# The last rows of a decoder block: norm vector multiplied in ahead, rstd and residual in one vector operation per half row

## The reference

```python
def rms_norm(x, g):
    xf = x.astype(jnp.float32)
    y = xf * lax.rsqrt(jnp.mean(xf * xf, axis=-1, keepdims=True) + EPS)
    return (y * g.astype(jnp.float32)).astype(x.dtype)
...
        h = rms_norm(x, g_pre_mlp[l]) * (1.0 + sc2) + sh2
        y = jnp.square(jax.nn.relu(h @ w_fc1[l])) @ w_fc2[l]
        x = x + gt2 * rms_norm(y, g_post_mlp[l])
```

## Time and profile before

| what | us |
|---|---|
| median of 3 runs (1533.65 to 1534.89) | 1533.8 |
| the profiled execution | 1535.47 |
| its span on the core | 1533.7 |
| PE busy in the span | 1429.6 |
| DVE busy | 1093.5 |
| ACT busy | 637.0 |
| POOL busy | 633.0 |

### The profile page before, as it was taken

How to read it: one execution, slowest core, us unless ns; L and a number is a source line. 1 busy time by engine, 2 the same in 40 slices (tenths; PEclk the granted TensorE clock), 3 DMA queues, 4 the chain that set the end, 5 groups by cost and what they waited for, 6 DMA issues and landing times.

```text
span 1533.7 us, 19644 instructions
## 1 busy us (share of the span) xinstructions
PE 1429.6 (93%) x7206; PEld 1196.2 (78%) x7206; DVE 1093.5 (71%) x1507; ACT 637.0 (42%) x1112; POOL 633.0 (41%) x541
## 2 busy tenths in 40 slices
PE   2897999999999999999999879999999989999992
PEld 2886777887888888888887767888888778888882
DVE  6759845678788888865414797777766788686857
ACT  2533524455666566652214552222224234242430
POOL 3315422233232232212214435766553844546457
PEclk9999999799999999999999989999999999999996
DMA  9388854122121111155542324444447453444332
GB/s 353 68 256 261 241 131 144 42 76 68 43 65 54 36 51 45 40 176 165 164 138 96 124 69 153 163 151 151 152 151 272 153 219 140 162 145 158 110 138 109
DMA packets 129702, 208.31 MB, mean 136 GB/s; under 512 B 19525, under 2 KB 84549, under 8 KB 126023
## 3 DMA queue, kind: packets, MB, share of 16 engines
q1 hardware_dynamic: 124874, 192.41, 38.4%
q0 software_dynamic: 4736, 14.68, 2.7%
HBM read 146.24 MB, written 54.53 MB: 131 GB/s over the span
## 4 chain that ended last, share of the span: by engine, by line
PE 78%; DVE 7%; POOL 4%; issue 3%; ACT 2%; SPq 2%; DMA 2%; POOLq 0%; DVEq 0%; ACTq 0%
PE ps L2005 17%; PE ps L2007 16%; PE ps L2006 16%; PE ps L2200 4%; PE ps L2011 4%; PE ps L2013 4%; PE ps L2012 4%; PE ps L2216 2%; PE ps L2167 2%; PE ps L2217 2%; PE ps L2168 2%; POOL x_in L1037 1%; DVE acc L1625 1%; SPq L538 1%; POOL hid L943 1%
## 5 line engine op out<-in xcount | busy, mean ns | idle before, releaser
L2005 PE MATMUL ps<-act_hi,a_hi 128*128 128x512 f32 x448 | 192.4, 429 | 1.4 <-DVE a_lo L1481 1.4
L2007 PE MATMUL ps<-act_hi,a_lo 128*128 128x512 f32 x448 | 176.0, 393 | 0.0
L2006 PE MATMUL ps<-act_lo,a_hi 128*128 128x512 f32 x448 | 175.8, 392 | 0.0
L861 POOL TENSOR_SCALAR ssum<-ssum 128x1 f32<-128x1 f32 (+1 forms) x160 | 42.7, 267 | 283.9 <-ACT p_win L1217 140.7
L1811 DVE TENSOR_TENSOR w_lo<-w1s,w_hi 128x1024 fp32r<-128x1024 f32 x54 | 101.5, 1887 | 51.0 <-ACT w_hi L1333 51.0
L920 POOL TENSOR_TENSOR w1s<-w1s 128x1024 f32<-128x1024 f32 x32 | 81.8, 2556 | 120.3 <-DMA w1s<-in_w_fc 72.0
L2005 PE MATMUL ps<-wr_hi,left_hi 128*128 128x512 f32 x320 | 125.4, 392 | 6.3 <-DVE y L1954 6.3
L2006 PE MATMUL ps<-wr_lo,left_hi 128*128 128x512 f32 x320 | 125.1, 391 | 0.0
L2007 PE MATMUL ps<-wr_hi,left_lo 128*128 128x512 f32 x320 | 125.0, 390 | 0.0
L1681 DVE TENSOR_TENSOR pt_lo<-ps,pt_hi 128x512 fp32r<-128x512 f32 (+1 forms) x160 | 103.3, 646 | 19.4 <-ACT pt_hi L1236 18.2
L1409 ACT ACTIVATE left_hi<-left_st 128x2048 fp32r<-128x2048 f32 x28 | 53.7, 1918 | 137.9 <-PE ps L2007 87.1
(11 more groups left out here) (277 smaller groups left out, 4078.7 us busy)
## 6 DMA issues: line engine op xcount, KB each, us to landing
left_st<-h_dram SPq DMA_DIRECT2D x28, 1024.0 KB, 4.9
ada<-in_w_ada SPq DMA_DIRECT2D x48, 512.0 KB, 5.8
h_dram<-hid SPq DMA_DIRECT2D x48, 512.0 KB, 3.1
w1s<-in_w_fc SPq DMA_DIRECT2D x32, 512.0 KB, 4.8
w2s<-in_w_fc SPq DMA_DIRECT2D x16, 1024.0 KB, 7.3
raw<-in_w_in SPq DMA_DIRECT2D x28, 512.0 KB, 4.2
g_dram<-g_out POOLq DMA_DIRECT2D x32, 256.0 KB, 2.4
mg<-g_dram SPq DMA_DIRECT2D x16, 512.0 KB, 3.9
```

The source lines that it names most:

```text
L2005: pe.matmul(dst, wh, mh, start=start, stop=False)
L2006: pe.matmul(dst, wh, ml, start=False, stop=False)
L2007: return pe.matmul(dst, wl, mh, start=False, stop=stop)
```

## The change

The scaling by rstd and v is taken apart. The multiplication by v comes first and needs no rstd: for y11 and y22 in place (`scale_early`, behind the squares that must read the old values), for y21 and y12 into u_3 and u_2, which are free by then (`scale_late`, behind the evacuation, while ACT squares the old values). Then one DVE operation per half row computes scaled * rstd + x1 into x1_in (`final`), and POOL's `add_x1` is gone. DVE runs these in the loop over the tiles of products 4, 5 and 6; `final` of one tile comes behind the evacuation and multiplication of the next. SP stores each half row (256 KB) by itself when it is made.

```diff
-        for n in range(TT):
-            a, t = 1 - n // 4, n % 4
-            sp.wait_ge(f_made, 2 * n + 2)
-            sp.dma_start(out_v[:, 4 * a + t, :], x1_in[a][:, t, :]).then_inc(out_st, 16)
-        sp.wait_ge(out_st, 16 * TT)
+        for n in range(2 * TT):
+            a, t, sl = 1 - n // TT, n // 2 % 4, slice((n % 2) * CH, (n % 2 + 1) * CH)
+            sp.wait_ge(f_made, n + 1)
+            sp.dma_start(out_v[:, 4 * a + t, sl], x1_in[a][:, t, sl]).then_inc(out_st, 16)
+        sp.wait_ge(out_st, 16 * 2 * TT)
...
-        def add_x1(a, t):
-
-            pool.wait_ge(pair_in[a], 16 * (TT + 4))
-            for half in range(2):
-                n = 2 * (4 * (1 - a) + t) + half
-                sl = slice(half * CH, (half + 1) * CH)
-                pool.wait_ge(f_scaled, n + 1)
-                pool.tensor_tensor(x1_in[a][:, t, sl], x1_in[a][:, t, sl], ((y11, y12), (y21, y22))[a][half][:, t, :],
-                                   ALU.add).then_inc(f_made, 1)
...
-        for n in range(TT + 1):
-            if n < TT:
-                final_rstd(1 - n // 4, n % 4)
-            if n:
-                add_x1(1 - (n - 1) // 4, (n - 1) % 4)
+        for n in range(TT):
+            final_rstd(1 - n // 4, n % 4)
...
-        def final_scale(a, t):
+        def scale_early(a, t):
+
+            src, half, squares = ((y11, 0, 1), (y22, 1, 5))[a]
+            dve.wait_ge(gt_in, 32)
+            dve.wait_ge(f_sq, squares + t)
+            dve.tensor_tensor(src[:, t, :], src[:, t, :], gt2[:, half * CH:(half + 1) * CH], ALU.mult).then_inc(f_scaled, 1)
+
+        def scale_late(a, t):
+
+            dst, src, half, part = ((u_2, y12, 1, 5), (u_3, y21, 0, 4))[a]
+            dve.wait_ge(part_made, e_count(FC2_CHUNKS - 1, part, t))
+            dve.tensor_tensor(dst[:, t, :], src[:, t, :], gt2[:, half * CH:(half + 1) * CH], ALU.mult).then_inc(f_scaled, 1)
+
+        def final(a, t):
 
             n = 4 * (1 - a) + t
-            r = stat[:, 32 + n:33 + n]
             dve.wait_ge(f_rstd, 2 * n + 2)
+            dve.wait_ge(pair_in[a], 16 * (TT + 4))
+            dve.wait_ge(f_scaled, 8 + n + 1)
             for half in range(2):
-                src = ((y11, y12), (y21, y22))[a][half][:, t, :]
-                dve.scalar_tensor_tensor(out=src, in0=src, scalar=r, in1=gt2[:, half * CH:(half + 1) * CH], op0=ALU.mult,
-                                         op1=ALU.mult).then_inc(f_scaled, 1)
+                src, sl = ((y11, u_2), (u_3, y22))[a][half], slice(half * CH, (half + 1) * CH)
+                dve.scalar_tensor_tensor(out=x1_in[a][:, t, sl], in0=src[:, t, :], scalar=stat[:, 32 + n:33 + n],
+                                         in1=x1_in[a][:, t, sl], op0=ALU.mult, op1=ALU.add).then_inc(f_made, 1)
...
-                if last and i == 6:
-                    final_scale(*((1, 2), (1, 3), (0, 0), (0, 1))[t])
+                if last and i == 4:
+                    scale_early(0, t)
+                    if t:
+                        scale_early(1, t - 1)
+                elif last and i == 5:
+                    if t == 0:
+                        scale_early(1, 3)
+                    scale_late(1, t)
+                    if t:
+                        final(1, t - 1)
+                elif last and i == 6:
+                    scale_late(0, t)
+                    if t:
+                        final(0, t - 1)
+                    else:
+                        final(1, 3)
...
-        final_scale(0, 2)
-        final_scale(0, 3)
+        final(0, 3)
```

## The result

The changed kernel takes 1514.2 us in the median of its runs (1510.4 to 1520.1), against 1534.4 us for the kernel before beside it: ratio 0.9874, 95% interval 0.9854 to 0.9893. On a second chip the ratio was 0.9889 (0.9861 to 0.9916), from three executions of the changed kernel; two more, of 2873 and 7286 us, were disturbed and are left out. It is faster by 1.1 to 1.3%.

What follows compares the result with a forecast made beforehand. The DVE-POOL relay was taken to bound the tail; DVE's new queue of 30.7 us from 1480.69, a 0.3 us rstd wait (1511.8) and 5.6 us behind it save 16.3 us from 1533.8: 1517.5 us, range 1515.0 to 1521.0.

Steps and rivals of the forecast that it cites:

- Bound: After PE's end: a relay of DVE scalings and POOL additions at 4.13 us a row, DVE slowed 1.1 us per operation.
- DVE's queue: From the first y22 evacuation at 1480.69: DVE's operations in one unbroken queue, 30.7 us, ending at 1511.5 before the rstd wait.
- Fused operations: On DVE at the end: 16 operations joining rstd and residual, 0.65 us start to start, 10.4 us.
- Self waits: On DVE: seven late multiplications wait for the evacuation directly in front, 0.12 us each, 0.9 us.
- Collision: Early y22 multiplications beside POOL's additions to y21: two slowed by 1.1 us each, 2.2 us; bounds one to four.
- The wait for the last rstd: At the last row, DVE waits for the square and two POOL operations: 0 to 1.2 us, taken as 0.3.
- the stores: Behind the last store's issue: 6.2 us to the span's end, less 0.6 for half rows, so 5.6 us.
- The signs: Expected in the new profile: POOL under 4 us after 1506, DVE without idle time, chain through DVE and PE.
- DVE at full length: Rival at the tail: DVE's operations run at full length and the late rstd waits; 1519.6 us, chance 0.22.
- the slow 1.75 us as DVE's own: Rival: slow scalings come from DVE's own work, not POOL; 32 operations cost 1.1 us more each, 1550.5 us, chance 0.04.
- The stores' split does nothing: Rival at the last store: the end stays 6.2 us behind the issue, through SP or the last half's receipt; 1518.1 us, chance 0.05.
- PE-bound: Rival at the end: DVE catches up and PE's last tile sets the end; 1515.4 us, chance 0.15.

Runs made afterwards that it cites:

- add_on_dve: Kernel before with the 16 residual additions moved from POOL to DVE, nothing multiplied ahead or fused, whole-row stores; ratio 0.9925.
- idle_adds: Changed kernel with POOL also making 16 additions of 128x512 on a tile nobody uses; ratio 1.0014 against the kernel before.
- whole_stores: Changed kernel with its output stored by whole rows of 512 KB instead of half rows; ratio 0.9903 against the kernel before.
- y11_earlier: Changed kernel with the four multiplications of y11 moved from product 4 to product 2; ratio 0.9881 against the kernel before.

## Why the prediction was right, step by step

- Bound: right that the relay of DVE and POOL was the tail (add_on_dve) and that POOL's work makes DVE's two-tensor operations slow (idle_adds). Too much was laid to DVE: the prediction says that DVE evacuates PE's last tiles late because it is slow, while POOL's queue was the full one and DVE waited for its rstd. By the estimate above the collision was about half of what moving the additions saves. The sum did not need this share, as it adds up the new queue and not the old one.
- DVE's queue: 31.1 us expected from the first evacuation of y22 to the last fused operation; 1472.79 to 1503.86 is 31.07. The parts hold one by one. Multiplications 0.60 to 0.61 start to start. Fused operations 0.66 (1492.65 to 1493.31). Self waits 0.11 each (1491.32 to 1492.04 is 0.72 where 0.60 to 0.61 is the pace without); the Trainium skill, "VectorE: DVE Perf Modes", section The DRAIN you can't avoid, has such a semaphore cost nothing extra, and this trace does not agree. Collision 2.2 expected; three multiplications took 1.10 and 2.81 us (for two) from start to start instead of 1.8 together, 2.1 more; by the sum it was two at full price, in fact two took 1.10 and one 1.7. The wait for the last rstd: 0.3 us expected; the row says 0.44, and 0.5 were lost from start to start. L1025 lasts 0.60 and L1028 0.94 us beside DVE, inside the bounds of the prediction.
- PE: not held up; its last matmul starts 28.0 us behind the mark, as before. The last evacuation 29.8 us behind the mark instead of 35.3.
- Loads of x1, gt2: no wait, as said.
- **The term that was mis-sized is the stores.** The prediction let the span end 6.2 us behind the last issue and took 0.6 us off for half rows. Measured: 4.7 us, 0.9 us less than 5.6, and for another reason. The 6.2 us belong to POOL's last operation, which in the kernel before happened to coincide with the last store's issue (1527.46 and 1527.49). The change moves POOL's end 1.45 us ahead of DVE's, and that is the whole of 6.2 - 4.7; the half rows themselves bring nothing (whole_stores). So the tail is 17.2 us shorter, against 16.3 forecast.
- The signs: POOL under 4 us at the end (3.09) and no idle time of DVE but at the last rstd came true. The chain was to run through DVE and PE; its last row runs through ACT and POOL's two small operations, since the last rstd holds the end, as the sum, though not the sign, had it.
- The rest of the first result goes with the clock: 1533.8 - 17.2 = 1516.6 us is what the change gives at the same mark; the four runs of the first result, at 1514.2 in the median, have a mean granted clock of 0.974 to 0.980, and that the rest comes from this was not tested. On the second chip the gap of the ratio, 1.1%, is 17 us.
- The rivals: DVE at full length, 1519.6, and the slow 1.75 us as DVE's own, 1550.5, are excluded. "The stores' split does nothing" (chance 0.05) came true in that half rows bring nothing, but neither its reason (SP or the last half's receipt) nor its price (the end stays 6.2 us behind the issue) did. PE-bound, 1515.4, is the closest: it would have had the same 5.6 us end; y11_earlier shows that PE's bound lies 1.4 us below the changed kernel.

## What to carry to other kernels

Two engines that pass rows to each other through on-chip memory may be slower than one of them alone: count an operation at the duration it has beside the other's, look for a row in which it runs alone, and see which of the two waits for the other. Before a time behind the last instruction is put down to a store, look which engine's end it follows in two kernels; if an earlier end of one engine shortens the span while the other engines and the stores end as before, what follows its last operation is the bound. When a profile of a changed kernel gains ahead of the change, mark an instruction that both have and compare from there, or a difference between executions is taken for a gain.

## What the runs showed of the hardware that was not expected

- The span ends 6.2 us behind GpSimd's last operation in nine traces of seven kernels, with tails of 37.5 to 56.6 us; behind VectorE's it can be 2.4 us. Moving one pair of 128x1 operations off GpSimd, with VectorE's end 0.3 us earlier, shortened the tail by 2.6 us.
- A 128x1 addition on GpSimd lasts 0.19 us where VectorE is idle, 0.60 us beside the fused operations, and 1.74 us in add_on_dve, where VectorE runs scalings and additions on SBUF tensors without a pause:

```profile
1515.23 1.74 POOL L1025 TENSOR_TENSOR col<-col 128x1 f32<-128x1 f32 x1 [0.76 <-ACT junk L1444]
1517.05 0.94 POOL L1028 TENSOR_TENSOR col<-col 128x1 f32<-128x1 f32 x1
```

- What a collision costs goes by position: in idle_adds the fused operations take 1.74 to 1.78 us, and the multiplication right before them, beside the same additions, 0.69 us, tile after tile. It need not be the full price: in the changed kernel two multiplications beside POOL's additions to y take 1.17 and 1.18 us.
- Splitting stores in half makes each land 0.6 us earlier (2.0 against 2.6 us behind the issue) and SP, with 0.33 us for each issue, keeps up; it moves the span only where the landing comes last.
